# A seventh place for expert down weights, in the room of two second buffers

## The reference, cut to what matters

```
def _hier_moe(h, ...):
    t = h.reshape(T, D)                       # 512 x 1024
    g_sel = top-1 of 4 groups; e_sel = top-2 of that group's 8 experts
    weights = g_top * e_top / sum(e_top)
    for e in range(32):
        hid = silu(t @ w_gate_exp[e]) * (t @ w_up_exp[e])      # 1024 -> 256
        y = y + combine[:, e:e + 1] * (hid @ w_down_exp[e])    # 256 -> 1024
```

## Time and profile before

| what | value |
|---|---|
| median of 3 runs | 661.6 us (660.67 to 663.9) |
| the profiled execution: its time | 659.75 us |
| its span, first to last instruction | 657.9 us |
| mean granted clock of TensorE | 0.989 of full speed |
| PE busy | 624.0 us (95%) |
| DVE, ACT, POOL busy | 375.8, 205.7, 101.3 us |
| bytes moved by the DMA engines | 174.44 MB |
| share of PE in the chain that ended last | 78% |

### The profile page before, as it was taken

How to read it: one execution, slowest core, us unless ns; L and a number is a source line. 1 busy time by engine, 2 the same in 40 slices (tenths; PEclk the granted TensorE clock), 3 DMA queues, 4 the chain that set the end, 5 groups by cost and what they waited for, 6 DMA issues and landing times.

```text
span 657.9 us, 7108 instructions
## 1 busy us (share of the span) xinstructions
PE 624.0 (95%) x2407; PEld 295.5 (45%) x2407; DVE 375.8 (57%) x717; ACT 205.7 (31%) x410; POOL 101.3 (15%) x96
## 2 busy tenths in 40 slices
PE   5899999999999999999999998989999999999882
PEld 4664444444444444556644564434343454433230
DVE  5948868998897753347852469743223242332056
ACT  5406534344444535521121350113122131222023
POOL 1007433300222320000000001021211212111001
PEclk9999999999999999999999998999999999999897
DMA  9996551514306080340497569699999999999997
GB/s 328 382 383 230 193 206 50 204 52 144 113 8 248 1 292 30 107 158 33 174 380 308 223 223 372 194 411 416 419 421 420 420 420 420 418 417 414 408 409 157
DMA packets 52135, 174.44 MB, mean 265 GB/s; under 512 B 9577, under 2 KB 9729, under 8 KB 41730
## 3 DMA queue, kind: packets, MB, share of 16 engines
q1 hardware_dynamic: 45024, 160.26, 62.8%
q0 software_dynamic: 6160, 12.10, 5.7%
q10 hardware_dynamic: 914, 1.61, 0.7%
HBM read 168.17 MB, written 15.21 MB: 279 GB/s over the span
## 4 chain that ended last, share of the span: by engine, by line
PE 78%; DVE 11%; DMA 4%; ACT 2%; issue 2%; SPq 1%; ACTq 0%; DVEq 0%
PE psum L820 17%; PE psum L1154 16%; PE psum L821 11%; PE psum L1215 9%; PE psum L1013 8%; DMA ring<-in_w_down_exp 2%; PE psum L1124 2%; PE psum L970 2%; PE psum L978 2%; PE psum L990 2%; SPq L591 1%; DVE score L1897 1%; DVE work L1585 1%; PE psum L953 1%; PE psum L944 1%
## 5 line engine op out<-in xcount | busy, mean ns | idle before, releaser
L820 PE MATMUL psum<-hT,ring 128*128 128x512 f32 (+1 forms) x320 | 135.6, 576 | 0.0
L820 PEld LDWEIGHTS psum<-hT,ring 128*128 128x128 f32 x320 | 59.4, 190 | 68.4 <-issue 60.1
L1154 PE MATMUL psum<-ring,hT 128*64 128x512 f32 (+2 forms) x320 | 87.0, 618 | 3.2 <-DMA ring<-in_w_up_exp 2.8
L821 PE MATMUL psum<-ring,hT 128*128 128x512 f32 x192 | 85.2, 597 | 0.0
L2018 DVE TENSOR_SCALAR work<-work 128x256 f32<-128x256 f32 x16 | 4.6, 290 | 95.4 <-PE psum L1164 69.6
L1567 DVE SCALAR_TENSOR_TENSOR rows<-ring,sm,rows 128x512 f32<-128x512 f32 x64 | 55.8, 872 | 1.7
L1357 ACT ACTIVATE both_bufs<-psum 32x512 f32<-32x512 f32 (+2 forms) x68 | 38.4, 564 | 58.8 <-PE psum L820 55.3
L821 PEld LDWEIGHTS psum<-ring,hT 128*128 128x128 f32 x192 | 35.6, 190 | 44.6 <-issue 44.2
L1463 ACT ACTIVATE work<-psum 128x256 f32<-128x256 f32 x17 | 6.5, 384 | 142.1 <-PE psum L1154 142.1
L1154 PEld LDWEIGHTS psum<-ring,hT 128*64 128x64 f32 (+2 forms) x320 | 28.5, 140 | 48.4 <-issue 47.1
L1215 PE MATMUL psum<-ring,work 128*64 128x512 f32 (+1 forms) x160 | 40.1, 597 | 1.2 <-ACT work L1469 1.2
(11 more groups left out here) (325 smaller groups left out, 902.2 us busy)
## 6 DMA issues: line engine op xcount, KB each, us to landing
ring<-in_w_down_exp SPq DMA_DIRECT2D x20, 1024.0 KB, 19.9
ring<-in_w_ada SPq DMA_DIRECT2D x8, 2048.0 KB, 13.2
ring<-in_w_in SPq DMA_DIRECT2D x7, 2048.0 KB, 8.9
ring<-in_w_gate_exp SPq DMA_DIRECT2D x12, 1024.0 KB, 20.5
ring<-in_w_up_exp SPq DMA_DIRECT2D x12, 1024.0 KB, 23.4
ring<-in_w_ada SPq DMA_DIRECT2D x16, 512.0 KB, 10.6
ring<-in_w_gate_exp SPq DMA_DIRECT2D x16, 512.0 KB, 12.7
ring<-in_w_up_exp SPq DMA_DIRECT2D x16, 512.0 KB, 13.8
```

The costliest lines, as they stand in the source:

```text
L820: return pe.matmul(o[:, at], w[:, k, b * P:(b + 1) * P], hT3[:, k, at], **ends)
L821: return pe.matmul(o[:, :], hT3[:, k, b * P:(b + 1) * P], w[:, k, :], **ends)
L1154: mm = pe.matmul(o[rows, :], XT[u % 2][:, k, rows], both(GU_SLOT[place])[:, k, :, :], start=(k == 0), stop=(k == KD - 1))
```

## The change

The change adds a seventh place for down weights. Its 1 MiB is taken from two buffers of 512 KiB: the second buffer of turned rows (`hT[:, 3D:4D]`, before `XT[1]`) and the second buffer of gathered rows (`work[:, 5D:6D]`, before `XG[1]`). So

- `XT` is one buffer. ACT's `turned(u)` waits for `gate_up(u-1)` (before: for `gate_up(u-2)`). `gate_up(1)` starts on the first half of its turned rows, as `gate_up(0)` did already.
- All gathers go to one buffer, but that of unit 1, which goes into room that the loop uses only later. POOL's `gather(u)` waits until `turn_x(u-1)` is done (before: `turn_x(u-2)`).
- Down position 6 is loaded ahead of the loop by SP, in two halves, once the router is done and the first gather has landed. Every load into this place is made in two halves, as the place is in two pieces.
- Down position p now takes the place of position p-7 instead of p-6: position 7 still waits for `down(0)`, 8 waits for `down(0)` instead of `down(1)`, 9 for `down(1)`, 10 for `down(1)` instead of `down(2)`, and so on. The order of SP's issues is otherwise kept.

```diff
-GU_SLOTS, DOWN_SLOTS = 7, 6
+GU_SLOTS, DOWN_SLOTS = 7, 7
+SPLIT = DOWN_SLOTS - 1
...
+        def down_part(s, i):
+            if s == SPLIT:
+                return (hT[:, 3 * D:4 * D], work[:, 5 * D:6 * D])[i]
+            return down_rows(s)[:, i * D:(i + 1) * D]
...
-        XG = [work[:, (4 + i) * D:(5 + i) * D] for i in range(GATHERS)]
-        XT = [hT[:, (2 + i) * KD * P:(3 + i) * KD * P].rearrange("p (k c) -> p k c", k=KD) for i in range(2)]
+        XT = hT[:, 2 * KD * P:3 * KD * P].rearrange("p (k c) -> p k c", k=KD)
+
+        def gathered(u):
+            return work[:, 2 * D:3 * D] if u == 1 else work[:, 4 * D:5 * D]
...
         def load_down(sp, e, s, signal):
-            sp.dma_start(down_rows(s), pick(wd_d, e)).then_inc(signal, 16)
+            if s == SPLIT:
+                for part in range(KF):
+                    load_down_half(sp, e, s, part, signal)
+            else:
+                sp.dma_start(down_rows(s), pick(wd_d, e)).then_inc(signal, 16)
...
             load_gate_up(sp, GU_SLOTS - 1, GU_SLOTS - 1, gu_in[GU_SLOTS - 1])
+            sp.wait_ge(router_done, NB)
+            sp.wait_ge(xg_in[0], 16)
+            load_down(sp, SPLIT, SPLIT, down_in[SPLIT])
...
             def gate_up(u):
-                pe.wait_ge(xt_ev, 2 * u + 1 if u == 0 else 2 * u + 2)
+                pe.wait_ge(xt_ev, 2 * u + 1 if u < FIRST_UNITS else 2 * u + 2)
...
                     if u == 0 and k == KD // 2:
                         turn_x(1)
-                        pe.wait_ge(xt_ev, 2)
+                    if u < FIRST_UNITS and k == KD // 2:
+                        pe.wait_ge(xt_ev, 2 * u + 2)
...
             def turned(u):
-                if u >= 2:
-                    act.wait_ge(gu_mm, u - 1)
+                if u >= 1:
+                    act.wait_ge(gu_mm, u)
...
             def gather(u):
                 if u >= GATHERS:
-                    pool.wait_ge(xt_mm, 2 * (u - GATHERS) + 2)
+                    pool.wait_ge(xt_mm, 2 * u)
```

More of the change, by code:

```diff
@@ L60 @@
 DOWN_SLOT = {p: POS[p] % DOWN_SLOTS for p in ORDER}
-DOWN_TURN = {p: POS[p] // DOWN_SLOTS for p in ORDER}
 GU_FREED = {p: UNIT_OF[ORDER[POS[p] - GU_SLOTS]] + 1 for p in ORDER[GU_SLOTS:]}
@@ L65 @@
 GU_LANDED = {p: sum(64 if q in SOON else 32 for q in ORDER[:POS[p] + 1] if GU_SLOT[q] == GU_SLOT[p]) for p in ORDER}
+HALVED = NU - 1
+DOWN_LANDED = {p: sum(32 if DOWN_SLOT[q] == SPLIT and q not in UNITS[HALVED] else 16 for q in ORDER[:POS[p] + 1]
+                      if DOWN_SLOT[q] == DOWN_SLOT[p]) + (16 if DOWN_SLOT[p] == SPLIT else 0) for p in ORDER}
 NT = NU + NOV
@@ L73 @@
 LAST_GU = {GU_SLOT[p]: UNIT_OF[p] for p in ORDER}
-SPARE_GU, SPARE_DOWN = RING, DOWN_SLOT[UNITS[NS - 1][0]]
-assert NS % 2 == 0 and all(LAST_GU[s] < NS for s in range(RING, GU_SLOTS)) and SPARE_DOWN < RING
+SPARE_GU, SPARE_DOWN = RING, RING + 1
+assert NS % 2 == 0 and all(LAST_GU[s] < NS for s in range(RING, GU_SLOTS))
+assert all(DOWN_SLOT[p] not in (SPARE_DOWN, SPLIT) for p in UNITS[HALVED])
 CHUNK = KD * 512
@@ L439, in build @@
         gu_rest = [sem(f"gu_rest{i}") for i in range(NU - HALVED)]
-        down_in = [sem(f"down_in{i}") for i in range(DOWN_SLOTS)]
+        down_in = [sem(f"down_in{i}") for i in range(SPLIT)] + [decay_in]
         down_rest = sem("down_rest")
@@ L763, in down_weights @@
                         load_down(sp, name(place), DOWN_SLOT[place], down_in[DOWN_SLOT[place]])
+                        del named[place]
             for u in range(FIRST_UNITS):
@@ L1153, in gate_up @@
                         rows = slice(h * n, (h + 1) * n)
-                        mm = pe.matmul(o[rows, :], XT[u % 2][:, k, rows], both(GU_SLOT[place])[:, k, :, :],
+                        mm = pe.matmul(o[rows, :], XT[:, k, rows], both(GU_SLOT[place])[:, k, :, :],
                                        start=(k == 0), stop=(k == KD - 1))
@@ L1179, in down_half @@
                         if i == 0:
-                            pe.wait_ge(down_in[DOWN_SLOT[place]], 16 * (DOWN_TURN[place] + 1))
+                            pe.wait_ge(down_in[DOWN_SLOT[place]], DOWN_LANDED[place])
                     if i == KF - 1:
@@ L1230, in overflow @@
                 pe.wait_ge(ov_x, o * 16 + 16)
-                rows = XG[0].rearrange("p (q k) -> p k q", k=KD)
+                rows = gathered(0).rearrange("p (q k) -> p k q", k=KD)
                 for k in range(KD):
@@ L1237, in overflow @@
                 for k in range(KD):
-                    mm = pe.matmul(ps[4][:, :], XT[0][:, k, :], both(SPARE_GU)[:, k, :, :], start=(k == 0),
+                    mm = pe.matmul(ps[4][:, :], XT[:, k, :], both(SPARE_GU)[:, k, :, :], start=(k == 0),
                                    stop=(k == KD - 1))
@@ L2221, in overflow @@
                 pool.sem_inc(pool_steps, 1)
-                g.indirect_dma_start(out=XG[0], out_offset=None, in_=h2_dram,
+                g.indirect_dma_start(out=gathered(0), out_offset=None, in_=h2_dram,
                                      in_offset=bass.IndirectOffsetOnAxis(ap=gix[:, 0:1], axis=0),
```

19 lines of the change are left out of this document (8 added, 11 removed).

## The result

The changed kernel takes 663.31 us, the median of 22 runs (661.66 to 666.18); the kernel before, beside it, 661.46 (22 runs, 659.74 to 663.99). The ratio is 1.0025, interval 1.0014 to 1.0037: **1.85 us slower**, within the 0.5% called no change, inside the range, but on the other side of the -0.3 us forecast. The profiled execution took 663.2 us, its span is 661.4.

A forecast was written before the change was run, and what follows sets the result against it. DMA transfers queued from about 417 us bound the loop: -2.5 us (down weight), +2.2 (pause), 0 (PE's waits) gave -0.3, so 659.4 us profiled, 661.3 median. Range 658.8 to 664.4; the forecast's own range 660.2 to 662.5.

The forecast's parts named there:

- What bounds the loop: Unit loop: ends when the transfer queue starting at about 417 us is worked off; PE has about 2.6 us margin.
- The load ahead, free in the gap: Gap before 417.5 us: one down weight moved there costs the loop nothing and removes 2.5 us of later transfers.
- The pause, 2.2 us within 1.7 to 2.7: Between about 444 and 448 us the DMA queue runs dry, costing 2.2 us, between 1.7 and 2.7.
- The moved gather: The gather issued at 438.59 comes at about 447 instead, taking 1.0 us of transfer out of the queue.
- PE's stand of 0.9 us: Before gate_up(1), PE waits 0.9 us for ACT's copy; counted as 0 at the end, covered by PE's margin.
- Gathers with one buffer less: From unit 4 on, gathers land in 7.3 to 8.7 us, inside 10.7 us, so PE waits for none.
- Unit 3's gather: Before turn_x(3), the tightest gather makes PE stand 0 to 0.4 us, up to 2.6 by the late value.
- The queue doesn't run dry: Rival, 444 to 448 us: engines still have work, so the 2.5 us stay won; median 659.1; chance 0.22.
- The load ahead buys nothing: Rival, 417.5 to 431 us: the gap's load is paid again, leaving the pause; median 663.3 to 664.3; chance 0.13.
- One buffer too few: Rival, units 3 on: gathers keep 10.9 us and hold PE up, +7.4 us, median 669.0; chance 0.10.
- The signs that were named: Checks: load in by 416.5 us, unit 16's wait about 1 us shorter, last down half within 1 us of 633.66.
- the second rival: The load ahead buys nothing: paid again in 417.5 to 431 us, median 663.3 to 664.3; chance 0.13.

The follow-up runs named there:

- the first two experiments: Changed kernel with down positions 7 and 8 issued together behind the halves, 660.74 us; changed kernel with position 6 loaded behind the halves, not ahead, 662.98 us.
- The late gathers alone: Kernel before, with only POOL's gather(u) waiting for turn_x(u-1) instead of turn_x(u-2): 662.75 us, ratio 1.0012.
- the late copy alone: Kernel before, with only turned(1) waiting for the end of gate_up(0), and gate_up(1) starting on half its rows: 662.24 us, ratio 1.0017.
- two down weights ahead: Changed kernel, with down positions 7 and 8 issued together right behind the loads in halves: 660.74 us, ratio 0.9987.
- the last experiment: Kernel with positions 7 and 8 issued together behind the halves, plus only position 11's expert number read ahead: 660.47 us, ratio 0.9984.

## Why the prediction came out on the other side

Its sum was -2.5 + 2.2 + 0 = -0.3. Measured, by the profiles: -2.5 + 4.4 + 0 = +1.9. Point by point:

- **What bounds the loop**: right. Transfers end it in the changed kernel as before, and what is lost around the pause comes out at the end of the loop nearly one for one.
- **The load ahead, free in the gap**: right. The share in the gap rose, loading position 6 twice cost nothing measurable, and one weight moved into the gap is worth 2.2 us between the first two experiments.
- **The pause, 2.2 us within 1.7 to 2.7**: place and mechanism were right (444 to 448 us was named), the term was mis-sized. This is the step that failed: it measured 4.4 us by bytes, 3.6 of them as missing share. It read the fill of the queue off two landings, 7.1 - 5.0 = 2.1 us. The trace has 16 landings for each load, one for each part of it, and the load is in with the last of them. In the changed kernel 15 parts of the one down weight in the queue were in from 444.69 to 445.76 us and the last at 447.27, where I had 447.3; the share had fallen to 0.59 with the others.

  The gate weight shows what the last landing hides. From the loop's start its 16 landings came at 39.7 us in the mean and 41.5 at the last before, and at 40.1 and 40.5 now. By the last the queue is 1.0 us ahead, near the 1.2 of the forecast; by the mean, which sets what is moved, it is 0.4 us behind, and the up weight behind it 1.0 (43.3 for 42.3).

  The other end came later: the gate weight was issued 447.86 - 412.45 = 35.41 us behind the loop's start, before 445.57 - 411.24 = 34.33; of that 1.1 us I had 0.9. The restart itself was priced rightly: the gate weight's last part was in at 452.92, 5.06 us after the issue, against the 5.0 of a lone load, and the 94 GB/s from 448 to 450 us lie within this time. The 4.4 us that the prediction set beside it are not for this load: the Trainium skill, "DMA: Bandwidth & Descriptors", section "Anatomy of one DMA", gives that fit for DMAs issued by POOL, and this one is SP's. Both bounds of the pause came from landings and shared the error.
- **The moved gather** was counted as 1.0 us inside that term. The late gathers alone lost 1.3 us in these 24 us, in their one profile, with a pause of only 0.1: a cost of that size seems to be there, as a lower rate of busy engines and not as idle ones.
- **PE's stand of 0.9 us**: the size was right (0.79), the zero beside it was not. PE's margin at unit 16 covered PE itself, but SP issues the loads of the loop's start behind PE's steps, so what makes PE late makes the queue late: with the late copy alone the gate weight was issued 447.09 - 411.75 = 35.34 us behind the loop's start, 1.0 later than before. I had counted that delay only at the pause. With nothing loaded ahead the two single buffers together lost 1.4 us by bytes; how much of it is PE's is not settled. The Trainium skill says in "Trainium Kernel Development and Optimization", section "Best Practices", to double-buffer so that DMA and compute overlap. The runs agree, and give the price that the prediction lacked, of both single buffers together: 1.2 us, ratio 1.0019 (1.0005 to 1.0034).
- **Gathers with one buffer less**: right in kind. PE waited for none from unit 4 on, since they landed sooner than the 10.1 us of before, as I had taken it. From the DMA issues of the changed kernel's loop (count, median us to landing):

```profile
work<-h_rows,tok_t POOLq DMA_INDIRECT x17, 8.1
```

- **Unit 3's gather**: no wait in the changed kernel, but 1.22 us with the late gathers alone and 1.27 with two down weights ahead, against the 0 to 0.4 I took and within the 2.6 of my bound.
- **The rivals.** "The queue doesn't run dry" fell: the share went to 0.04. "The load ahead buys nothing" gave nearly the right number, 663.3 to 664.3, for a wrong reason: the gap's load isn't paid again up to 431 us (the first 23.8 us went at 373 GB/s, and at 362 with the weight loaded twice, against 366), the pause was larger. "One buffer too few" fell as priced (669.0); what single buffers cost is 1.2 us.
- **The signs that were named.** The load ahead was in at 417.83, not 416.5; the loop began 1.2 us later, and its first half load was issued at 417.63. The wait before unit 16's first weights was to be 1 us shorter and was 0.8 longer, and PE's start on the last down half was to be within 1 us of 633.66 and was 3.15 behind, 1.2 of it from the loop's later start: both because the transfers, not PE, had become later.
- **The range** held the time only because it reached to the second rival; the forecast's own range, to 662.5, did not.

## What to carry to other kernels

Before you take a load out of a queue, ask how full the queue is when the next one is issued, in bytes not yet moved, not by when the last load lands. Where it can run dry, moving a load forward wins only if the next load's issue is moved forward as well: the same change cost 1.9 us with the queue left to run dry, and won 2.4 and 3.3 with two loads issued together and gate/up 11 in halves. A buffer given up for room is costed twice, once for who waits for it and once for which issues stand behind that wait.

## What was not expected of the hardware

TensorE's granted clock fell near unit 16 in some profiles and not in others, and the length of the wait doesn't sort them. Behind 2.58 us of waiting 32 matmuls took 5.34 us in the kernel before, behind 3.36 us the same ones took 3.64 us in the changed kernel, and behind 2.31 us 5.34 us again in the last experiment. Its window there has the granted clock in the last number but two:

```profile
624.00:626.00 2.00, 2.00 (x16) 0.56 (x12) 0.00 (x0) 0.00 (x0) 0.00 (x0) 0.50 1.02 406
```

At 1.2 GHz the group costs 1.7 us more. In the kernel before that lies under a transfer; in the last experiment it took PE's margin.

And a queue that has run dry doesn't restart with the issue: issued at 447.86, the changed kernel's loads give 0.56 of busy share and 94 GB/s from 448 to 450 us. The 5.06 us to the gate weight's landing have this slow start in them.
